# Splitting each chunk of two expert tables by one 1024-wide instruction instead of two 512-wide ones

## The chip and what is measured

The kernel runs on one core of a Trainium2 chip. The metric is the device time of one execution in microseconds. A core has the engines TensorE (PE in the rows; its weight loads are PEld), VectorE (DVE), ScalarE (ACT), GpSimd (POOL) and SyncE (SP, which here issues the transfers), each with its own instruction stream. They wait for one another on semaphores.

## The reference

One layer of a small diffusion backbone on 256 tokens of width 1024: projections and attention first, then the part that this study is on, a retrieval feed-forward over 16384 experts:

```
s = jnp.einsum('thpd,hpkd->thpk', q, sub_keys)        # 8 heads x 2 lists x 128 keys
top_s, top_i = lax.top_k(s, 16)                        # then the 16 best of 16 x 16 pairs
best_s, best_pos = lax.top_k(cand_s, 16)
g = jax.nn.softmax(best_s, axis=-1)
act = jax.nn.gelu(einsum('thkd,td->thk', u_tab[expert], hb))
return einsum('thk,thkd->td', g * act, v_tab[expert])
```

## The kernel before

It doesn't gather. It goes over both tables whole (64 MB each), in 128 chunks of 128 experts x 1024 values, and gives an expert that wasn't chosen the weight zero. All of it is fp32. To have nearly fp32 accuracy at the speed of the reduced fp32 format, each matrix is split into a high part (rounded) and a low part (the rest), and each product is three matmuls: hi x hi, hi x lo, lo x hi.

A chunk's way, in the names of the code:
- SyncE brings it from HBM into `stage`, which has four slots of [128, 1024]. A slot is filled again once the low part of the chunk in it is made (`lo_made`).
- ScalarE rounds it into `hi` (`round_chunk`, L939), when `stage_full` of the slot has come and TensorE has consumed what stood there (`piece_done`).
- VectorE subtracts into `lo` (`rest`, L1306), once `hi_made` has come.
- TensorE uses both and counts `piece_done`.

`hi` and `lo` hold four pieces of 512 columns each, so two chunks. Three stretches follow one another:
- **u**, chunks 0 to 63 of the first table: 24 matmuls of 256 columns a chunk (`u_chunk`, L788 to L790), and ScalarE's gelu on the chunk before the last (L1062). VectorE finds the top 16 of heads 4 to 7 between chunks (`choose`), then decodes them to expert numbers by 2048-wide instructions (L1454, L1459, L1463) with two chunks between each, and the softmax comes at the end.
- **u beside gates**, chunks 64 to 127: the same, and before each chunk four products that spread the gates over all experts (`gates`, L798), for which ScalarE and VectorE build one-hot rows (L1081, L1087, L1495).
- **v**, the 128 chunks of the second table: 12 matmuls of 512 columns a chunk (`v_chunk`, L851 to L853), which add up over all chunks in four banks. The weights of this product, gates times gelu, are split too, into `w_hi` (ScalarE, L1117) and `w_lo` (VectorE, L1535), two chunks deep, shown as h_hi and h_lo in the rows.

The order on each engine is written out by hand in the code; in the loops it is the order of the statements, and each engine runs its own in order.

Of the kernel before, what the change touches and what calls it, by code (L numbers as in the profile page):

```python
# [1 line left out]

# [28 lines left out]
LOWEST = -3.0e38  # L51
SLOTS = 4
CHUNKS = NK
PIECE = D // 2
PIECES = 4
GT = 4
GROUPS = T // GT

# [197 lines left out]
def build(nc, x_t, ctx_t, cols, rows, sgu_gain, final_gain, constants, sgu_wt, bias_mask, ada_w, w_in,  # L256
# [21 lines left out]
    with ExitStack() as stack:  # L278
# [82 lines left out]
        bias = sbuf("stage", [P, SLOTS, D])  # L361
        stage = bias
        BM = bias[:, :, :].rearrange("p s d -> p (s d)").rearrange("p (h b n) -> p h b n", h=HEADS, b=TB)
        hi = sbuf("hi", [P, PIECES, PIECE], F32R)
        lo = sbuf("lo", [P, PIECES, PIECE], F32R)
        h2_hi = sbuf("h2_hi", [P, KD, T], F32R)
        h2_lo = sbuf("h2_lo", [P, KD, T], F32R)
        with ExitStack() as views:
# [103 lines left out]
        @block.sync  # L472
        def _(sp):
            sp.dma_start(colv[:, :], cols).then_inc(cols_in, 16)
            sp.dma_start(X1, x_t).then_inc(x_in, 16)
            sp.dma_start(con[:, :], constants).then_inc(consts_in, 16)
            for n, (matrix, b) in enumerate(blocks):
                late = (matrix, b) in rings[1]
                slot = ring_of[(matrix, b)]
                if slot >= RING:  # L480
                    old = place[last_read(rings[late][slot - RING])]
                    sp.wait_ge(bank_full[old[0]], old[1] + 1)
                elif late:
                    old = place[("attend", 3)]
                    sp.wait_ge(bank_full[old[0]], old[1] + 1)
                sp.dma_start((WR2 if late else WR)[:, slot % RING], sources[matrix][b])\
                  .then_inc(ring_full[late][slot % RING], 16)
                if n == 2 * RING + 1:
                    sp.dma_start(C0, ctx_t).then_inc(ctx_in, 16)
                if n == RING - 1:  # L490
                    sp.dma_start(sgb_row, rows[:, 0:SGU_G * P]).then_inc(gating_in, 16)
                    sp.dma_start(sg_gain, sgu_gain).then_inc(gating_in, 16)
                    sp.dma_start(swt, sgu_wt).then_inc(gating_in, 16)

                if (matrix, b) == ("w_q", PH - 1):
                    old, use = place[("w_q", 2)]
                    sp.wait_ge(bank_full[old], use + 1)
                    for j in range(SLOTS):
                        sp.dma_start(stage[:, j, :], peer_u_t[j]).then_inc(stage_full[j], 16)
                if n == 27:  # L500
                    sp.dma_start(BM, bias_mask).then_inc(bias_in, 16)
                    sp.wait_ge(h_ready, KD)
                    sp.dma_start(SK, subkeys_t).then_inc(subkeys_in, 16)
                if (matrix, b) == ("w_q", 0):
                    sp.wait_ge(yr_ready, 1)
                    sp.dma_start(g2_row, rows[:, SGU_G * P:]).then_inc(g2_row_in, 16)
            with sp.Fori(1, CHUNKS // SLOTS) as i:
                for j in range(SLOTS):
                    sp.wait_ge(lo_made, i * (2 * SLOTS) + (2 * (j + 1 - SLOTS)))
                    sp.dma_start(stage[:, j, :], peer_u_t[i * SLOTS + j]).then_inc(stage_full[j], 16)  # L510
            with sp.Fori(0, CHUNKS // SLOTS) as i:
                for j in range(SLOTS):
                    sp.wait_ge(lo_made, i * (2 * SLOTS) + (2 * (CHUNKS + j + 1 - SLOTS)))
                    sp.dma_start(stage[:, j, :], v_rows[i * SLOTS + j]).then_inc(stage_full[j], 16)
            sp.wait_ge(gates_done, GROUPS)
            sp.dma_start(fin, final_gain).then_inc(fin_in, 16)
            for n in range(2 * TB):
                tb, half = n // 2, slice(n % 2 * 512, n % 2 * 512 + 512)
                sp.wait_ge(out_ready, n + 1)
                sp.dma_start(out[tb * P:(tb + 1) * P, half], x1n[:, tb, half]).then_inc(stored, 16)  # L520
            sp.wait_ge(stored, 16 * 2 * TB)
# [3 lines left out]
        def _(pe):  # L525
# [255 lines left out]

            def u_chunk(j, c):
                o = bank[j % SLOTS][:, 0:T]
                for h in range(2):
                    pe.wait_ge(lo_made, c * 2 + (h + 1))
                    for n in range(KD // 2):
                        k, p, kk = KD // 2 * h + n, (2 * j + h) % PIECES, slice(n * P, (n + 1) * P)
                        pe.matmul(o, hi[:, p, kk], h2_hi[:, k, :], start=(k == 0), stop=False)  # L788
                        pe.matmul(o, hi[:, p, kk], h2_lo[:, k, :], start=False, stop=False)  # L789
                        mm = pe.matmul(o, lo[:, p, kk], h2_hi[:, k, :], start=False, stop=(k == KD - 1))  # L790
                    mm.then_inc(piece_done, 1)


            def gates(j, g):
# [46 lines left out]
            def v_chunk(j, v, first=False, last=False):  # L841
                pe.wait_ge(wlo_made, v + 1)

                order = [(tb, half) for half in range(2) for tb in range(TB)]
                for n, (tb, half) in enumerate(sorted(order) if last else order):
                    if last or n % TB == 0:
                        pe.wait_ge(lo_made, v * 2 + (2 * CHUNKS + half + 1))
                    p = (2 * j + half) % PIECES
                    o = bank[4 + 2 * tb + half][:, :]
                    tt = slice(tb * P, (tb + 1) * P)  # L850
                    pe.matmul(o, w_hi[:, j % 2, tt], hi[:, p, :], start=first, stop=False)  # L851
                    pe.matmul(o, w_hi[:, j % 2, tt], lo[:, p, :], start=False, stop=False)  # L852
                    mm = pe.matmul(o, w_lo[:, j % 2, tt], hi[:, p, :], start=False, stop=last)  # L853
                    if last:
                        mm.then_inc(out_full, 1)
                    elif n % TB == TB - 1:
                        mm.then_inc(piece_done, 1)

            pe.wait_ge(gated, GROUPS)
            pe.wait_ge(choice_t_ready, 2 * TB)  # L860
# [27 lines left out]
        def _(act):  # L888
# [42 lines left out]
            def round_chunk(j, use, done=None):  # L931


                for h in range(2):
                    if done is not None:
                        act.wait_ge(piece_done, done + h)
                    if h == 0:
                        act.wait_ge(stage_full[j], use)
                    act.activation(hi[:, (2 * j + h) % PIECES, :], stage[:, j, h * PIECE:(h + 1) * PIECE], ACT.Copy)\  # L939
                       .then_inc(hi_made, 1)  # L940

            def round_h2(k):
                act.wait_ge(h2_ready, k + 1)
# [126 lines left out]

            def u_steps(i, j):

                round_chunk(j, i * 16 + 16, i * (2 * SLOTS) + (2 * j - 3))
                gelu_chunk(j - 2, i * SLOTS + (j - 2))

            def one1_squares(j, g, reused=True):
# [10 lines left out]
                act.activation(ONE1[:, j % 2], ONE1[:, j % 2], ACT.Relu, bias=1.0, scale=-1.0).then_inc(one1_made, 1)  # L1087

            for c in (2, 3):
                round_chunk(c, 16, 2 * c - 3)  # L1090
                gelu_chunk(c - 2, c - 2)
            with act.Fori(1, DECODE_UNTIL // SLOTS) as i:
                for j in range(SLOTS):
# [7 lines left out]
            for j in range(SLOTS):  # L1101
                c = MERGE + j
                one1_squares(j, j, reused=j >= 2)
                round_chunk(j, 16 * (c // SLOTS) + 16, 2 * c - 3)
                one1_rest(j, j)
                if j < 2:
                    gelu_chunk(j + 2, c - 2)
# [2 lines left out]
            with act.Fori(1, (CHUNKS - MERGE) // SLOTS) as i:  # L1110
                for j in range(SLOTS):
                    one1_squares(j, i * SLOTS + j)
                    round_chunk(j, i * 16 + (16 * (MERGE // SLOTS) + 16), i * (2 * SLOTS) + (2 * (MERGE + j) - 3))
                    one1_rest(j, i * SLOTS + j)
                    gelu_beside(j + 2, i * SLOTS + (j - 2))
            def w_round(j, v):
# [2 lines left out]

            for j in range(2):  # L1120
                n = CHUNKS + j
                round_chunk(j, 16 * (n // SLOTS) + 16, 2 * n - 3)
                gelu_beside(j + 2, n - 2 - MERGE)
                if j == 0:

                    act.wait_ge(gated, GROUPS)
                    act.wait_ge(piece_done, 2 * CHUNKS)
                w_round(j, j)


            act.wait_ge(multiplied, CHUNKS - MERGE)
            for v in (2, 3):
                act.wait_ge(piece_done, 2 * (CHUNKS + v - 1))
                w_round(v, v)
                round_chunk(v, 16 * (CHUNKS // SLOTS) + 16, 2 * (CHUNKS + v) - 3)
            with act.Fori(1, CHUNKS // SLOTS) as i:
                for j in range(SLOTS):
                    act.wait_ge(piece_done, i * (2 * SLOTS) + 2 * (CHUNKS + j - 1))
                    w_round(j, i * SLOTS + j)
                    round_chunk(j, i * 16 + (16 * (CHUNKS // SLOTS) + 16), i * (2 * SLOTS) + (2 * (CHUNKS + j) - 3))  # L1140

# [12 lines left out]
        def _(dve):  # L1156
# [143 lines left out]


            def rest(j, c):
                for h in range(2):
                    p = (2 * j + h) % PIECES
                    dve.wait_ge(hi_made, c * 2 + (h + 1))
                    dve.tensor_tensor(lo[:, p, :], stage[:, j, h * PIECE:(h + 1) * PIECE], hi[:, p, :].bitcast(F32),  # L1306
                                      ALU.subtract).then_inc(lo_made, 1)

            for kind, n in steps:
                if kind == "group" and n < 2:  # L1310
# [363 lines left out]
```

## Time and profile before

| what | value |
|---|---|
| median of 3 runs | 1107.93 us (1102.68 to 1108.59) |
| span of the profiled execution | 1106.2 us |
| its own time | not recorded apart from the span |
| TensorE busy | 1072.4 us, 97% of the span |
| VectorE busy | 760.1 us, 69% |
| ScalarE busy | 628.5 us, 57% |
| on the chain that ended last | TensorE 92%, ScalarE 3%, transfers 2%, VectorE 2% |

The chain that ended last is followed back from the last instruction, at each step to what released it. Busy time of TensorE is modelled from starts and a pipeline's length, so a matmul of 256 columns is shown as 0.28 us while the next one starts 0.12 us after it.

### The profile page before, as it was taken

What the parts mean: (1) busy time and instruction counts of PE and PEld (TensorE: products, weight loads), DVE (VectorE), ACT (ScalarE), POOL (GpSimd) and SP (SyncE); (2) the same over time, 40 slices, a digit from 0 to 9 for tenths busy, and PEclk for the clock granted to TensorE, in tenths of its full rate; (3) what the DMA queues carried; (4) which work ended last, traced back from release to release, by engine and by line L of the source; (5) the groups of instructions that cost most, each with busy time, mean ns of one, the idle gap of its engine ahead of it and who ended that gap; (6) DMA issues with size and microseconds to landing.
All of it is one profiled execution on the core that took longest, in us unless ns stands there. A gap on an engine that the chain in (4) does not pass through costs nothing.

```text
span 1106.2 us, 22735 instructions
## 1 busy us (share of the span) xinstructions
PE 1072.4 (97%) x7358; PEld 962.5 (87%) x7358; DVE 760.1 (69%) x1660; ACT 628.5 (57%) x1319; POOL 37.1 (3%) x11
## 2 busy tenths in 40 slices
PE   5899999999999999999999999999999999999996
PEld 3687986797999999999999999997888888888885
DVE  1373145576988878868888888886666666666666
ACT  2452235545345555578888888875555555555554
POOL 0000000003340000020000000000000000000000
PEclk9698998999999999999999999999999999999998
DMA  9665741044525555555344344445555666666653
GB/s 362 274 234 197 268 159 57 1 154 152 228 78 190 175 188 173 187 183 161 133 140 144 133 140 144 133 133 174 196 197 192 190 191 192 194 197 192 190 191 113
DMA packets 45547, 191.65 MB, mean 173 GB/s; under 512 B 5186, under 2 KB 5314, under 8 KB 38980
## 3 DMA queue, kind: packets, MB, share of 16 engines
q1 hardware_dynamic: 45508, 191.11, 50.9%
q8 instruction: 26, 0.43, 0.2%
q14 instruction: 13, 0.11, 0.0%
HBM read 190.04 MB, written 1.05 MB: 173 GB/s over the span
## 4 chain that ended last, share of the span: by engine, by line
PE 92%; ACT 3%; DMA 2%; DVE 2%; POOL 0%; issue 0%; DVEq 0%; SPq 0%; ACTq 0%
PE bank L788 11%; PE bank L789 11%; PE bank L790 11%; PE bank L851 10%; PE bank L853 10%; PE bank L852 10%; PE bank L798 5%; PE bank L546 3%; PE bank L547 3%; PE bank L548 3%; PE bank L669 2%; PE bank L566 1%; PE bank L652 1%; PE bank L651 1%; PE bank L660 1%; PE bank L556 1%
## 5 line engine op out<-in xcount | busy, mean ns | idle before, releaser
L939 ACT ACTIVATE hi<-stage 128x512 fp32r<-128x512 f32 x512 | 305.7, 622 | 119.6 <-PE bank L790 119.5
L1306 DVE TENSOR_TENSOR lo<-stage,hi 128x512 fp32r<-128x512 f32 x512 | 336.2, 695 | 33.9 <-ACT hi L939 31.4
L788 PE MATMUL bank<-h_hi,hi 128*128 128x256 f32 x1024 | 295.1, 288 | 1.0 <-ACT A L1062 1.0
L790 PE MATMUL bank<-h_hi,lo 128*128 128x256 f32 x1024 | 289.6, 283 | 0.0
L789 PE MATMUL bank<-h_lo,hi 128*128 128x256 f32 x1024 | 289.5, 283 | 0.0
L851 PE MATMUL bank<-hi,h_hi 128*128 128x512 f32 x512 | 199.3, 389 | 1.2 <-DVE h_lo L1535 1.2
L853 PE MATMUL bank<-hi,h_lo 128*128 128x512 f32 x512 | 199.2, 389 | 0.0
L852 PE MATMUL bank<-lo,h_hi 128*128 128x512 f32 x512 | 199.2, 389 | 0.0
L788 PEld LDWEIGHTS bank<-h_hi,hi 128*128 128x128 f32 x1024 | 196.1, 192 | 1.1 <-ACT A L1062 1.1
L789 PEld LDWEIGHTS bank<-h_lo,hi 128*128 128x128 f32 x1024 | 196.3, 192 | 0.0
L790 PEld LDWEIGHTS bank<-h_hi,lo 128*128 128x128 f32 x1024 | 196.0, 191 | 0.0
L1117 ACT ACTIVATE h_hi<-A 128x256 fp32r (+1 forms) x128 | 53.5, 418 | 162.4 <-PE bank L853 159.5
L1535 DVE TENSOR_TENSOR h_lo<-A,h_hi 128x256 fp32r<-128x256 f32 x128 | 54.5, 426 | 129.4 <-ACT h_hi L1117 129.4
L851 PEld LDWEIGHTS bank<-hi,h_hi 128*128 128x128 f32 x512 | 96.1, 188 | 21.2 <-issue 1.4
L852 PEld LDWEIGHTS bank<-lo,h_hi 128*128 128x128 f32 x512 | 96.1, 188 | 20.1
L853 PEld LDWEIGHTS bank<-hi,h_lo 128*128 128x128 f32 x512 | 96.1, 188 | 19.9
L1081 ACT ACTIVATE gate_buf<-con,choice_t 128x128 f32<-128x128 f32 x256 | 81.2, 390 | 0.0
L548 PE MATMUL bank<-h_hi,ring_low 128*128 128x256 f32 x256 | 72.6, 284 | 0.0
L1495 DVE TENSOR_SCALAR gate_buf<-con,choice_t 128x128 f32<-128x128 f32 x256 | 71.0, 340 | 0.0
L798 PE MATMUL bank<-gate_buf 128*128 128x128 f32 x512 | 67.6, 275 | 0.0
L798 PEld LDWEIGHTS bank<-gate_buf 128*128 128x128 f32 x512 | 62.8, 192 | 0.0
L1503 DVE TENSOR_TENSOR A<-A,bank 128x512 f32 (+1 forms) x64 | 43.9, 687 | 10.4 <-PE bank L798 1.8
(222 smaller groups left out, 1365.8 us busy)
## 6 DMA issues: line engine op xcount, KB each, us to landing
stage<-in_peer_u_t SPq DMA_DIRECT2D x128, 512.0 KB, 3.3
stage<-in_peer_v SPq DMA_DIRECT2D x128, 512.0 KB, 3.6
A<-in_ada_w SPq DMA_DIRECT2D x24, 1024.0 KB, 7.5
A<-in_w_in SPq DMA_DIRECT2D x11, 1024.0 KB, 4.8
A<-in_w_q SPq DMA_DIRECT2D x8, 1024.0 KB, 5.2
A<-in_w_out SPq DMA_DIRECT2D x4, 1024.0 KB, 7.3
stage<-in_bias_mask SPq DMA_DIRECT2D x1, 2048.0 KB, 12.9
A<-in_x_t SPq DMA_DIRECT2D x1, 1024.0 KB, 5.3
```

The costliest lines, as they stand in the source:

```text
L548: mm = pe.matmul(o, a_lo, b_hi, start=False, stop=(k == KD - 1))
L788: pe.matmul(o, hi[:, p, kk], h2_hi[:, k, :], start=(k == 0), stop=False)
L789: pe.matmul(o, hi[:, p, kk], h2_lo[:, k, :], start=False, stop=False)
L790: mm = pe.matmul(o, lo[:, p, kk], h2_hi[:, k, :], start=False, stop=(k == KD - 1))
L798: mm = pe.matmul(bank[4 + j][:, t * NK:(t + 1) * NK], ONE1[:, j, t, :], ONE2[:, j, t, :], start=True, stop=True)
L851: pe.matmul(o, w_hi[:, j % 2, tt], hi[:, p, :], start=first, stop=False)
L852: pe.matmul(o, w_hi[:, j % 2, tt], lo[:, p, :], start=False, stop=False)
L853: mm = pe.matmul(o, w_lo[:, j % 2, tt], hi[:, p, :], start=False, stop=last)
L939: act.activation(hi[:, (2 * j + h) % PIECES, :], stage[:, j, h * PIECE:(h + 1) * PIECE], ACT.Copy)\
L1081: last = act.activation(ONE1[:, j % 2, t, :], iota, ACT.Square, bias=choice_t[:, 0, bass.ds(g * GT + t, 1)])
L1306: dve.tensor_tensor(lo[:, p, :], stage[:, j, h * PIECE:(h + 1) * PIECE], hi[:, p, :].bitcast(F32), ALU.subtract).then_inc(lo_made, 1)
L1495: last = dve.tensor_scalar(ONE2[:, j % 2, t, :], iota, choice_t[:, 1, bass.ds(tt, 1)], choice_t[:, 2, bass.ds(tt, 1)], ALU.is_equal, ALU.mult)
```

## The change

Each chunk is rounded by one 1024-wide instruction and its rest is taken by one 1024-wide instruction. `hi` and `lo` are two tiles of a whole chunk, in the same space. The semaphores `hi_made`, `lo_made` and `piece_done` count chunks, where they counted halves. The matmuls, their order in a chunk but for which tile they name, and everything else stay.

```diff
-PIECE = D // 2
-PIECES = 4
+TILES = 2
-        hi = sbuf("hi", [P, PIECES, PIECE], F32R)
-        lo = sbuf("lo", [P, PIECES, PIECE], F32R)
+        hi = sbuf("hi", [P, TILES, D], F32R)
+        lo = sbuf("lo", [P, TILES, D], F32R)
@@ SyncE
-                    sp.wait_ge(lo_made, i * (2 * SLOTS) + (2 * (j + 1 - SLOTS)))
+                    sp.wait_ge(lo_made, i * SLOTS + (j + 1 - SLOTS))
@@ TensorE, u_chunk
-                for h in range(2):
-                    pe.wait_ge(lo_made, c * 2 + (h + 1))
-                    for n in range(KD // 2):
-                        k, p, kk = KD // 2 * h + n, (2 * j + h) % PIECES, slice(n * P, (n + 1) * P)
-                        pe.matmul(o, hi[:, p, kk], h2_hi[:, k, :], start=(k == 0), stop=False)
-                        pe.matmul(o, hi[:, p, kk], h2_lo[:, k, :], start=False, stop=False)
-                        mm = pe.matmul(o, lo[:, p, kk], h2_hi[:, k, :], start=False, stop=(k == KD - 1))
-                    mm.then_inc(piece_done, 1)
+                pe.wait_ge(lo_made, c + 1)
+                for k in range(KD):
+                    kk = slice(k * P, (k + 1) * P)
+                    pe.matmul(o, hi[:, j % TILES, kk], h2_hi[:, k, :], start=(k == 0), stop=False)
+                    pe.matmul(o, hi[:, j % TILES, kk], h2_lo[:, k, :], start=False, stop=False)
+                    mm = pe.matmul(o, lo[:, j % TILES, kk], h2_hi[:, k, :], start=False, stop=(k == KD - 1))
+                mm.then_inc(piece_done, 1)
@@ TensorE, v_chunk
+                pe.wait_ge(lo_made, v + (CHUNKS + 1))
-                    if last or n % TB == 0:
-                        pe.wait_ge(lo_made, v * 2 + (2 * CHUNKS + half + 1))
-                    elif n % TB == TB - 1:
-                        mm.then_inc(piece_done, 1)
+                if not last:
+                    mm.then_inc(piece_done, 1)
@@ ScalarE, round_chunk
-                for h in range(2):
-                    if done is not None:
-                        act.wait_ge(piece_done, done + h)
-                    if h == 0:
-                        act.wait_ge(stage_full[j], use)
-                    act.activation(hi[:, (2 * j + h) % PIECES, :], stage[:, j, h * PIECE:(h + 1) * PIECE], ACT.Copy)\
-                       .then_inc(hi_made, 1)
+                if done is not None:
+                    act.wait_ge(piece_done, done)
+                act.wait_ge(stage_full[j], use)
+                act.activation(hi[:, j % TILES, :], stage[:, j, :], ACT.Copy).then_inc(hi_made, 1)
@@ ScalarE, u: first half needs piece 2c-3, now the whole needs chunk c-1 of the count
-                round_chunk(j, i * 16 + 16, i * (2 * SLOTS) + (2 * j - 3))
+                round_chunk(j, i * 16 + 16, i * SLOTS + (j - 1))
@@ VectorE, rest
-                for h in range(2):
-                    p = (2 * j + h) % PIECES
-                    dve.wait_ge(hi_made, c * 2 + (h + 1))
-                    dve.tensor_tensor(lo[:, p, :], stage[:, j, h * PIECE:(h + 1) * PIECE], hi[:, p, :].bitcast(F32),
-                                      ALU.subtract).then_inc(lo_made, 1)
+                dve.wait_ge(hi_made, c + 1)
+                dve.tensor_tensor(lo[:, j % TILES, :], stage[:, j, :], hi[:, j % TILES, :].bitcast(F32),
+                                  ALU.subtract).then_inc(lo_made, 1)
```

What stands on ScalarE in one turn of the loop of v, before (ISA is a separate instruction that only waits):

```order
L1117 ISA [waits piece_done]
L1117 ACTIVATE h_hi<-A 128x256
L936 REGISTER_ALU
L939 ACTIVATE hi<-stage 128x512 [waits stage_full1,piece_done]
L939 ACTIVATE hi<-stage 128x512 [waits piece_done]
```

And in the changed kernel (its line numbers are lower, since blank lines at its head are gone):

```order
L1112 REGISTER_ALU
L1091 ISA [waits piece_done]
L1091 ACTIVATE h_hi<-A 128x256
L914 ACTIVATE hi<-stage 128x1024 [waits stage_full1,piece_done]
L1112 REGISTER_ALU
```

Two instructions became one; the wait for consumed weights still stands ahead of all of them.

On VectorE, in the decoding at the end of u, four halves (two chunks) stand between two 2048-wide instructions before:

```order
L1454 TENSOR_TENSOR A<-A,con 128x2048
L1306 TENSOR_TENSOR lo<-stage,hi 128x512 [waits hi_made,dve_done]
L1306 TENSOR_TENSOR lo<-stage,hi 128x512 [waits hi_made] x3
L1459 TENSOR_TENSOR A<-A 128x2048
L1306 TENSOR_TENSOR lo<-stage,hi 128x512 [waits hi_made,dve_done]
```

In the changed kernel these four are two 1024-wide ones, at the same place.

## Rows read from the trace of the kernel before

**Rows 1.** The page's first line.

```profile
span 1106.2 us, 22735 instructions
```

**Rows 2.** Windows: stretch, length; busy PE, PEld, DVE, ACT, POOL; clock; DMA share; GB/s.

```profile
319.00:500.00 181.00, 180.03 (x1502) 179.86 (x1502) 148.62 (x352) 102.77 (x193) 13.90 (x2) 1.00 0.54 176
500.00:747.00 247.00, 246.84 (x2097) 246.63 (x2095) 216.61 (x514) 201.60 (x518) 0.00 (x0) 1.00 0.43 140
748.00:1095.00 347.00, 346.94 (x1531) 287.40 (x1532) 217.52 (x383) 186.64 (x383) 0.00 (x0) 1.00 0.59 189
```

**Rows 3.** Groups by form: count, busy us, mean ns, idle before.

```profile
L939 ACT ACTIVATE hi<-stage 128x512 fp32r<-128x512 f32 x512 | 305.7, 622 | 119.6 <-PE bank L790 119.5
L956 ACT ACTIVATE hi<-A 128x2048 fp32r<-128x2048 f32 x6 | 11.5, 1912 | 18.5 <-DMA A<-in_w_in 18.4
L1240 DVE TENSOR_TENSOR ring_low<-A,hi 128x2048 fp32r<-128x2048 f32 x6 | 13.8, 2292 | 39.6 <-ACT hi L956 39.5
```

**Rows 4.** Timeline of v, one turn: start, length, engine, line, idle before.

```profile
851.83 0.42 ACT L1117 ACTIVATE h_hi<-A 128x256 fp32r x1 [1.26 <-PE bank L853]
852.15 1.14 ACT L939 ACTIVATE hi<-stage 128x512 fp32r<-128x512 f32 x2
852.80 1.29 DVE L1306 TENSOR_TENSOR lo<-stage,hi 128x512 fp32r<-128x512 f32 x2
854.25 0.39 PE L851 MATMUL bank<-hi,h_hi 128*128 128x512 f32 x1
...
854.55 0.42 ACT L1117 ACTIVATE h_hi<-A 128x256 fp32r x1 [1.26 <-PE bank L853]
```

**Rows 5.** Timeline of u, in the decoding.

```profile
448.24 0.69 DVE L1306 TENSOR_TENSOR lo<-stage,hi 128x512 fp32r<-128x512 f32 x1 [0.34 <-ACT hi L939]
448.85 2.29 DVE L1454 TENSOR_TENSOR A<-A,con 128x2048 f32<-128x2048 uint32 x1
...
450.45 0.63 ACT L939 ACTIVATE hi<-stage 128x512 fp32r<-128x512 f32 x1 [0.81 <-PE bank L790]
451.17 2.08 DVE L1306 TENSOR_TENSOR lo<-stage,hi 128x512 fp32r<-128x512 f32 x3
...
453.13 0.28 PE L788 MATMUL bank<-h_hi,hi 128*128 128x256 f32 x1
...
453.33 0.63 ACT L939 ACTIVATE hi<-stage 128x512 fp32r<-128x512 f32 x1 [0.81 <-PE bank L790]
```

**Rows 6.** Timeline of VectorE in u, around one step of top-k.

```profile
388.37 0.08 DVE L1265 MATCH_VALUE_LOAD top_i<-top_v,A 128x8 f32 x1
...
390.46 1.28 DVE L1306 TENSOR_TENSOR lo<-stage,hi 128x512 fp32r<-128x512 f32 x2
```

**Rows 7.** Timeline of u, where TensorE waited.

```profile
329.10 2.83 DVE L1306 TENSOR_TENSOR lo<-stage,hi 128x512 fp32r<-128x512 f32 x2
...
332.11 0.36 PE L788 MATMUL bank<-h_hi,hi 128*128 128x256 f32 x1 [0.97 <-ACT A L1062]
...
332.31 0.28 PE L789 MATMUL bank<-h_lo,hi 128*128 128x256 f32 x1
```

**Rows 8.** Timeline of the stage before u, a wait of TensorE.

```profile
256.03 0.42 DVE L1401 TENSOR_TENSOR h_lo<-A,h_hi 128x256 fp32r<-128x256 f32 x1
...
256.50 0.39 PE L546 MATMUL bank<-h_hi,query_hi 128*128 128x256 f32 x1
```

**Rows 9.** Timeline of ScalarE in u, around the softmax.

```profile
479.02 1.28 ACT L939 ACT_TABLE_LOAD   x1
...
489.41 1.28 ACT L939 ACT_TABLE_LOAD   x1 [0.61 <-PE bank L790]
```

**Rows 10.** Timeline of u beside gates.

```profile
603.75 0.63 ACT L939 ACTIVATE hi<-stage 128x512 fp32r<-128x512 f32 x1 [0.65 <-PE bank L790]
...
604.36 0.36 PE L788 MATMUL bank<-h_hi,hi 128*128 128x256 f32 x1
```

**Rows 11.** Transfers of the page: count, KB each, us from issue to landing.

```profile
stage<-in_peer_v SPq DMA_DIRECT2D x128, 512.0 KB, 3.6
```

More of the change, by code:

```diff
@@ L512, in _ @@
                 for j in range(SLOTS):
-                    sp.wait_ge(lo_made, i * (2 * SLOTS) + (2 * (CHUNKS + j + 1 - SLOTS)))
+                    sp.wait_ge(lo_made, i * SLOTS + (CHUNKS + j + 1 - SLOTS))
                     sp.dma_start(stage[:, j, :], v_rows[i * SLOTS + j]).then_inc(stage_full[j], 16)
@@ L842, in v_chunk @@
                 pe.wait_ge(wlo_made, v + 1)
+                pe.wait_ge(lo_made, v + (CHUNKS + 1))
                 order = [(tb, half) for half in range(2) for tb in range(TB)]
-                for n, (tb, half) in enumerate(sorted(order) if last else order):
-                    if last or n % TB == 0:
-                        pe.wait_ge(lo_made, v * 2 + (2 * CHUNKS + half + 1))
-                    p = (2 * j + half) % PIECES
+                for tb, half in sorted(order) if last else order:
+                    dd = slice(half * 512, half * 512 + 512)
                     o = bank[4 + 2 * tb + half][:, :]
                     tt = slice(tb * P, (tb + 1) * P)
-                    pe.matmul(o, w_hi[:, j % 2, tt], hi[:, p, :], start=first, stop=False)
-                    pe.matmul(o, w_hi[:, j % 2, tt], lo[:, p, :], start=False, stop=False)
-                    mm = pe.matmul(o, w_lo[:, j % 2, tt], hi[:, p, :], start=False, stop=last)
+                    pe.matmul(o, w_hi[:, j % 2, tt], hi[:, j % TILES, dd], start=first, stop=False)
+                    pe.matmul(o, w_hi[:, j % 2, tt], lo[:, j % TILES, dd], start=False, stop=False)
+                    mm = pe.matmul(o, w_lo[:, j % 2, tt], hi[:, j % TILES, dd], start=False, stop=last)
                     if last:
                         mm.then_inc(out_full, 1)
-                    elif n % TB == TB - 1:
-                        mm.then_inc(piece_done, 1)
+                if not last:
+                    mm.then_inc(piece_done, 1)
             pe.wait_ge(gated, GROUPS)
@@ L1089, in _ @@
             for c in (2, 3):
-                round_chunk(c, 16, 2 * c - 3)
+                round_chunk(c, 16, c - 1)
                 gelu_chunk(c - 2, c - 2)
@@ L1103, in _ @@
                 one1_squares(j, j, reused=j >= 2)
-                round_chunk(j, 16 * (c // SLOTS) + 16, 2 * c - 3)
+                round_chunk(j, 16 * (c // SLOTS) + 16, c - 1)
                 one1_rest(j, j)
@@ L1112, in _ @@
                     one1_squares(j, i * SLOTS + j)
-                    round_chunk(j, i * 16 + (16 * (MERGE // SLOTS) + 16), i * (2 * SLOTS) + (2 * (MERGE + j) - 3))
+                    round_chunk(j, i * 16 + (16 * (MERGE // SLOTS) + 16), i * SLOTS + (MERGE + j - 1))
                     one1_rest(j, i * SLOTS + j)
@@ L1121, in _ @@
                 n = CHUNKS + j
-                round_chunk(j, 16 * (n // SLOTS) + 16, 2 * n - 3)
+                round_chunk(j, 16 * (n // SLOTS) + 16, n - 1)
                 gelu_beside(j + 2, n - 2 - MERGE)
@@ L1126, in _ @@
                     act.wait_ge(gated, GROUPS)
-                    act.wait_ge(piece_done, 2 * CHUNKS)
+                    act.wait_ge(piece_done, CHUNKS)
                 w_round(j, j)
@@ L1132, in _ @@
             for v in (2, 3):
-                act.wait_ge(piece_done, 2 * (CHUNKS + v - 1))
+                act.wait_ge(piece_done, CHUNKS + v - 1)
                 w_round(v, v)
-                round_chunk(v, 16 * (CHUNKS // SLOTS) + 16, 2 * (CHUNKS + v) - 3)
+                round_chunk(v, 16 * (CHUNKS // SLOTS) + 16, CHUNKS + v - 1)
             with act.Fori(1, CHUNKS // SLOTS) as i:
                 for j in range(SLOTS):
-                    act.wait_ge(piece_done, i * (2 * SLOTS) + 2 * (CHUNKS + j - 1))
+                    act.wait_ge(piece_done, i * SLOTS + (CHUNKS + j - 1))
                     w_round(j, i * SLOTS + j)
-                    round_chunk(j, i * 16 + (16 * (CHUNKS // SLOTS) + 16), i * (2 * SLOTS) + (2 * (CHUNKS + j) - 3))
+                    round_chunk(j, i * 16 + (16 * (CHUNKS // SLOTS) + 16), i * SLOTS + (CHUNKS + j - 1))
             act.activation(fsum[:, 2, TB:TB + 1], eps[:, :], ACT.Sqrt)
```

## The prediction

> **What bounds the kernel now.** I read the windows by stage first. The end of the kernel is made of three long stretches [rows 2]: u, chunks 0 to 63 of the first table (319 to 500 us); u beside gates, chunks 64 to 127 (500 to 747); v, the 128 chunks of the second table (748 to 1095). TensorE is busy for 180.03 of 181, 246.84 of 247 and 346.94 of 347 us, at a granted clock of 1.00, while ScalarE and VectorE have gaps everywhere. So TensorE sets the time, and it is idle for 0.97 + 0.16 + 0.06 = 1.2 us in all. Nothing that the split into parts costs now is on the path; the question is only whether it stays off.
>
> The timeline then tells how close it is. hi and lo hold two chunks, so chunk c can be rounded only once chunk c-2 has been consumed, and it must be ready when chunk c-1 is consumed. In v [rows 4] ScalarE is released by chunk v-2 at 851.83, does the weight tile w_hi (0.32 us until the next starts), then both halves of hi from 852.15; VectorE starts lo at 852.80; TensorE starts chunk v at 854.25. The next turn starts at 854.55, so a chunk takes 2.72 us. Between release and need there are 854.25 - 851.83 = 2.42 us. In u [rows 5] they are 453.13 - 450.45 = 2.68 us, and a chunk takes 24 matmuls of 0.12 us, 2.88 us (450.45 to 453.33, the next release).
>
> **What the change removes and adds.** By pieces, hi's second half runs on ScalarE while lo's first half runs on VectorE, and TensorE needs only lo's first half to begin. Whole chunks put the full hi and the full lo one behind the other ahead of TensorE. In u they also take away an early start: so far the first half is released half a chunk sooner, when half of chunk c-2 is consumed.
>
> Duration of the new instructions. No row has a 1024-wide one. On a line between the 512-wide and the 2048-wide rows [rows 3], ScalarE: 0.622 + (1.912 - 0.622)/3 = 1.05 us; VectorE, from the single lo of 0.69 us [rows 5]: 0.69 + (2.292 - 0.69)/3 = 1.22 us. Bounds: not under the start-to-start time of halves, not over two halves back to back (1.14 and 1.29 us, [rows 4]). The first lo starts 0.03 us after the first hi ends (852.15 + 0.62).
>
> TensorE's restart. In v it hardly ever waits, so I take it from the one wait on lo in u [rows 7]: lo ends at 329.10 + 2.83 = 331.93, the matmul starts at 332.11, and the one after it at 332.31, 0.08 later than the 0.12 of a running row. Together 0.26 us. The lower bound is in an earlier stage [rows 8]: VectorE ends at 256.45, TensorE starts at 256.50 with a matmul of 0.39 where 0.28 is usual, together 0.16. I take 0.26: same line, same kind of wait, inside a loop.
>
> **v.** From release to TensorE's start: 0.32 + 1.05 + 0.03 + 1.22 + 0.26 = 2.88 us, where 2.42 are to be had. Late by 0.46 us. The wait ties chunk v to the end of chunk v-2, so the delay comes once in two chunks: 63 pairs x 0.46 = **29.0 us**. With 0.16 for the restart 0.36 x 63 = 23; with nothing for it 0.20 x 63 = 13.
>
> In v ScalarE and VectorE are busy for 187 and 218 of 347 us [rows 2]. The Trainium skill (Perfetto Trace Analysis, Optimizing Scalar/DVE Operations) says that grouping operations helps where such an engine is saturated, and that where it is not but causes bubbles elsewhere, breaking instructions up lets work be done sooner. This change goes against the second half of it. By that rule too the time rises; how much, the page doesn't say, and the sum is from the rows alone.
>
> **u.** With VectorE free: 1.05 + 0.03 + 1.22 + 0.26 = 2.56 us against 2.68, so 0.12 us are left and nothing is lost. But VectorE is not always free. Its lo of chunk c would end at 450.45 + 2.30 = 452.75. Then
> - decoding: a 2048-wide instruction follows every two chunks, 12 in all (L1454, L1459 and L1463, four each). It starts 0.08 before the end of the lo ahead (448.85 against 448.24 + 0.69) and the next lo 2.32 after it (451.17), [rows 5]. Then lo of chunk c+1 ends at 452.67 + 2.32 + 1.22 = 456.21, TensorE starts by 456.47, and needed it at 453.13 + 2.88 = 456.01. 12 x 0.46 = **5.5 us**. Now the first half of that lo is the one needed, half a chunk's time ahead of it, and this hides it.
> - top-k: the longest of the eight steps of a head takes 2.09 us (388.37 to 390.46, [rows 6]); by the same sum 0.23 us late, for 4 heads **0.9 us**. The other steps are short enough.
> - ScalarE's table loads around the softmax. hi is due on a beat of 2.88 us from 450.45: at 479.25 and at 490.77. The first is held up by a load until 479.02 + 1.28 = 480.30 [rows 9], and by 1.05 - 0.62 = 0.43 more since the hi ahead is longer: 1.48 - 0.12 = 1.4 us. The second load stands between the wait and hi, 1.28 - 0.12 = 1.2 us. Together **2.5 us**. Today they fall on a first half with half a chunk to spare.
>
> Sum of u: 8.9 us. Below it the restart of 0.16 gives 12 x 0.36 + 0.5 + 2.3 = 7. Above it: if the chain in u is over 0.12 us longer than I have it, nearly every pair of its 64 chunks waits. At 0.3 us late this is 32 x 0.3 = 10 us more.
>
> **u beside gates.** hi is released at 603.75 and chunk c-1 starts at 604.36 [rows 10]. lo is done and TensorE could start at 603.75 + 2.56 = 606.31; TensorE is on chunk c-1 until 604.36 + 2.88 = 607.24 and then has gates. 0.9 us to spare without the gates. ScalarE and VectorE there are busy 202 and 217 of 247 us, and each loses a start per chunk. Nothing, either way.
>
> **Transfers.** A slot of stage is released when the whole lo is made, before and after; that comes some 0.4 us later. There are four slots and a transfer takes 3.6 us [rows 11] out of the three chunk times (over 8 us) that it has. Hidden.
>
> **Sum.** 29.0 + 8.9 = 37.9 us. The profiled execution's span is 1106.2 us [rows 1]; the median of three runs is 1107.9, 1.7 above it, which I put to what lies around the span. 1106.2 + 37.9 + 1.7 = 1145.8 us, say 1146 (+3.4%). The runs of before spread over 5.9 us, so about 0.5% is what can be told from no change.
>
> **The rivals.**
> - *The chain fits in v: no change.* If hi and lo together take no more than 2.42 us from release, TensorE never waits in v. It decides at 0.46 less than my 2.88: the restart at nothing (0.26) and 0.20 off the two instructions. The start-to-start times speak a little for it (a lo starts 0.60 after the one ahead though it is shown as 0.69). Then u's few waits stay at most: 1108 to 1115 us. For 1108 sharp, within 0.5%, u's have to vanish too. 11% in all, 4 of them for the second.
> - *Saved starts pay: as now or faster.* Per chunk ScalarE saves 1.14 - 1.05 = 0.09 us and VectorE 0.07. This pays only where TensorE waits for them, and that is 1.2 us in 775 [rows 2]: 1106 to 1108 us. Against it: that idle time is all there is to win. 3%. The Trainium skill (VectorE: DVE Perf Modes, on the TRN2 errata) says that each instruction pays a fixed extra latency, and advises large tiles. The fixed part agrees with the rows (two halves cost more than the whole on the line); the advice, by the idle time above, buys nothing here.
> - *u is tied as well.* The 0.12 us of u are used up (one loop turn in four starts hi behind a separate waiting instruction, which is new to the path): 10 us more, 1156 us. 15%.
> - *The clock falls.* If TensorE's gaps of 0.46 us in 5.9 brought the granted clock below 1.00, v alone would grow by tens of us. Against it: the gaps stay short, and TensorE is busy over 90% of the time. 2%.
> - My forecast, v tied pairwise and u at a few places: 69%.
>
> **How the numbers follow.** The likeliest case with its bounds runs from 1107.9 + 13 + 5 = 1126 to 1107.9 + 29 + 9 + 4 = 1150; the one tied in u reaches to 1160. I leave out the two rivals at 1115 and below and the clock, 16% in all, so the range is 1127 to 1160. Slower by over 0.5%: 69 + 15 + 2 and most of the 7, 0.91; within 0.5%: 0.07; faster: 0.02.
>
> **What would show it.** ScalarE's 1024-wide hi at 1.05 us and VectorE's lo at 1.22. In v, TensorE waits for VectorE's lo some 63 times (or 126 times, half as long), 15 to 29 us in all by idle time alone, and a pair of chunks takes 5.90 us where it took 5.44; VectorE no longer idles beside a full TensorE. In u, waits at the 12 decoding instructions and at two table loads, and a plain chunk still at 2.88 us. u beside gates keeps its 247 us within 1. The prediction is wrong if the pair in v stays at 5.44 (the chain is shorter than the rows say), or if plain chunks of u stretch.

## The result: 2.9% slower

Before 1107.1 us (median), after 1138.0: a ratio of 1.0289, 95% interval 1.0256 to 1.0322. The forecast was 1146 in 1127 to 1160.

The profiled execution went from 1106.2 to 1134.5 us. Its page's lines that answer to [rows 1] and [rows 3], for the changed kernel:

```profile
span 1134.5 us, 21582 instructions
...
PE 73%; DVE 11%; ACT 9%; DMA 3%; issue 3%; ACTq 0%; POOL 0%; DVEq 0%; SPq 0%
...
L1278 DVE TENSOR_TENSOR lo<-stage,hi 128x1024 fp32r<-128x1024 f32 x256 | 314.8, 1230 | 119.6 <-ACT hi L914 119.0
L914 ACT ACTIVATE hi<-stage 128x1024 fp32r<-128x1024 f32 x256 | 269.1, 1051 | 142.7 <-PE bank L768 142.6
```

512 instructions of each engine became 256, and their busy time fell: ScalarE's from 305.7 to 269.1 us, VectorE's from 336.2 to 314.8. Yet the time rose. The chain that ended last was TensorE to 92% before; now it is TensorE to 73%, and ScalarE and VectorE hold 20% of it: making hi and lo has become work that the end of the program waits for.

Where it came from is read from the first and the last start of TensorE's lines. For the changed kernel (columns: least, median and greatest length in ns, then first and last start):

```profile
L766 PE MATMUL bank<-h_hi,hi x1024: 277/283/388, 316.5 to 748.9; 128*128 128x256 f32 x171
L776 PE MATMUL bank<-gate_buf x512: 272/275/275, 508.2 to 746.3; 128*128 128x128 f32 x171
L828 PE MATMUL bank<-hi,h_hi x512: 387/393/504, 750.6 to 1124.0; 128*128 128x512 f32 x171
```

u runs from the first of these to the second, and so on. The same three lines give every kernel of this study a length for each stretch:

| kernel | u | u beside gates | v |
|---|---|---|---|
| before | 186.2 | 242.5 | 347.5 |
| changed | 191.7 (+5.5) | 242.4 | 373.4 (+25.9) |

Together 31.3 us more. The part of the program ahead of u took 319.4 us in one profile and 316.5 in the other; over all profiles here it lies between 313.7 and 322.4 whatever the kernel, so single spans differ by some us for that alone, and the lengths of the stretches are the sharper measure (the same kernel parts agree within 0.1 or 0.2 us). The granted clock goes with it. In the profile of the kernel before it falls from 1.00 (2.4 GHz) to 0.50 (1.2 GHz) for 10 us from 168 us on. In that of the changed kernel it doesn't, though TensorE had been busy for 9.50 of the 10 us from 155 to 165 in both. The eight profiles with such a drop between 166 and 185 us start u at 317.3 us or later, the four without it at 316.5 or earlier.

The waits of TensorE after 320 us, longest first (us in total, times, longest):

```profile
PEld bank L828 <- DVE lo L1278: 33.5, 83, 0.5
...
PEld bank L766 <- DVE lo L1278: 2.9, 10, 0.6
PE bank L766 <- DVE lo L1278: 2.8, 4, 1.1
```

These are shown at the weight loads (PEld), which stand first at a chunk; before the change no such row named lo. The weight loads' idle time is more than what TensorE lost. The starts of v's 1536 matmuls, set against those of the kernel before, show 63 late starts, one at the head of every second chunk, and 14.8 us lost at them in all.

One pair of chunks in v, in the timeline of the changed kernel, answers to [rows 4]:

```profile
853.18 0.42 ACT L1091 ACTIVATE h_hi<-A 128x256 fp32r x1 [1.78 <-PE bank L830]
853.50 1.04 ACT L914 ACTIVATE hi<-stage 128x1024 fp32r<-128x1024 f32 x1
...
854.58 1.23 DVE L1278 TENSOR_TENSOR lo<-stage,hi 128x1024 fp32r<-128x1024 f32 x1 [0.42 <-ACT hi L914]
...
855.40 0.39 PE L830 MATMUL bank<-hi,h_lo 128*128 128x512 f32 x1
855.86 0.50 PE L828 MATMUL bank<-hi,h_hi 128*128 128x512 f32 x1
856.20 0.40 PE L829 MATMUL bank<-lo,h_hi 128*128 128x512 f32 x1
...
861.75 0.50 PE L828 MATMUL bank<-hi,h_hi 128*128 128x512 f32 x1
```

Read it as a relay. TensorE's end of a chunk releases ScalarE at 853.18; w_hi (h_hi in the row) comes first; hi from 853.50 to 854.54; lo from 854.58 to 855.81; TensorE starts 0.05 us later, at 855.86. It would have been ready one spacing after 855.40, at 855.63. The next such start is at 861.75: this pair takes 5.89 us, where one took 5.44. It is one of the longer ones; the mean of v's 63 pairs is 0.41 us above 5.44.

### The profile page after: what moved, and what is told of

It reads as the page before. It is cut to its first block, busy times and chain, and to the rows that moved or that the text cites. A ratio compares the mean times of both kernels' runs of the same rounds, so it can differ in the third digit from the quotient of the medians.

```text
span 1134.5 us, 21582 instructions
## 1 busy us (share of the span) xinstructions
PE 1092.9 (96%) x7358; PEld 952.6 (84%) x7358; DVE 742.6 (65%) x1404; ACT 598.3 (53%) x1063; POOL 37.0 (3%) x11
## 3 DMA queue, kind: packets, MB, share of 16 engines
HBM read 190.04 MB, written 1.05 MB: 168 GB/s over the span
## 4 chain that ended last, share of the span: by engine, by line
PE 73%; DVE 11%; ACT 9%; DMA 3%; issue 3%; ACTq 0%; POOL 0%; DVEq 0%; SPq 0%
PE bank L766 10%; PE bank L767 9%; PE bank L768 9%; DVE lo L1278 7%; PE bank L828 7%; PE bank L830 6%; PE bank L829 6%; ACT hi L914 6%; PE bank L776 5%; PE bank L525 3%; PE bank L527 3%; PE bank L526 3%; PE bank L648 1%; DMA A<-in_w_in 1%; PE bank L545 1%
## 5 line engine op out<-in xcount | busy, mean ns | idle before, releaser
L1278 DVE TENSOR_TENSOR lo<-stage,hi 128x1024 fp32r<-128x1024 f32 x256 | 314.8, 1230 | 119.6 <-ACT hi L914 119.0
L914 ACT ACTIVATE hi<-stage 128x1024 fp32r<-128x1024 f32 x256 | 269.1, 1051 | 142.7 <-PE bank L768 142.6
L828 PE MATMUL bank<-hi,h_hi 128*128 128x512 f32 x512 | 207.9, 406 | 5.9 <-DVE h_lo L1507 1.2
```

The lines of the kernel that those rows point to most:

```text
L828: pe.matmul(o, w_hi[:, j % 2, tt], hi[:, j % TILES, dd], start=first, stop=False)
L914: act.activation(hi[:, j % TILES, :], stage[:, j, :], ACT.Copy).then_inc(hi_made, 1)
L1278: dve.tensor_tensor(lo[:, j % TILES, :], stage[:, j, :], hi[:, j % TILES, :].bitcast(F32), ALU.subtract).then_inc(lo_made, 1)
```

## The experiments

**Theory 1** is that of the prediction: the full hi and the full lo stand one behind the other between the end of chunk c-2 and the need for chunk c, and this relay is longer than what TensorE has to do meanwhile. **Theory 2** has several forms: it is the coarser waiting and releasing by chunks, or one engine's long instruction by itself, or a disturbance of TensorE beside the relay. Ratios are to the kernel before, run on the same chip. The edits are against the changed kernel where nothing else is said.

### Only lo by halves

```diff
-                pe.wait_ge(lo_made, c + 1)
                 for k in range(KD):
+                    if k % (KD // 2) == 0:
+                        pe.wait_ge(lo_made, c * 2 + (k // (KD // 2) + 1))
...
-                dve.tensor_tensor(lo[:, j % TILES, :], stage[:, j, :], hi[:, j % TILES, :].bitcast(F32),
-                                  ALU.subtract).then_inc(lo_made, 1)
+                for s in (slice(0, D // 2), slice(D // 2, D)):
+                    dve.tensor_tensor(lo[:, j % TILES, s], stage[:, j, s], hi[:, j % TILES, s].bitcast(F32),
+                                      ALU.subtract).then_inc(lo_made, 1)
```

(and the same wait in v and on SyncE.)

> hi by one 1024-wide instruction as in the change, lo by two halves, TensorE waits by halves; TensorE's count of consumed chunks stays whole. Theory 1 (hi and lo stand one behind the other between the end of chunk v-2 and the need for chunk v): in v 0.32 + 1.05 + 0.04 + 0.69 + 0.05 = 2.15 us of 2.42, no wait; in u only the two table loads may still cost some 0.5 us each. 1107 to 1110 us. Theory 2 (the coarser release of consumed chunks, or the longer ScalarE instruction, costs it): both are still there, so most of the 31 us stay, 1125 to 1138.

Measured: 1108.3 us, ratio 1.0006 (0.9990 to 1.0022). u 188.0, v 347.7. ScalarE's single instruction and the release by chunks are still there and cost nothing in v. u keeps 1.8 us, where theory 1 had some 0.5 at each of two table loads. Its starts show 0.8 at the first table load (481.48) and nothing at the second; 0.5 at 446.07, where a 2048-wide reduce and three short VectorE instructions stand ahead of lo; and 0.4 more at the start of 330.41, at which the kernel before waits too (332.11). So the total lies in theory 1's range, and its places in u are right in part.

### Only hi by halves

```diff
-                act.activation(hi[:, j % TILES, :], stage[:, j, :], ACT.Copy).then_inc(hi_made, 1)
+                for s in (slice(0, D // 2), slice(D // 2, D)):
+                    act.activation(hi[:, j % TILES, s], stage[:, j, s], ACT.Copy).then_inc(hi_made, 1)
...
-                dve.wait_ge(hi_made, c + 1)
+                dve.wait_ge(hi_made, c * 2 + 2)
```

> The other way round: hi by two halves, lo by one 1024-wide instruction after both, all else as in the change. Theory 1: the chain has 1.14 us where it had 1.05, so 0.09 us more in each of 63 pairs and a little in u: 1138 + 6 = 1144 us, slower than the change. Theory 2 (the single long ScalarE instruction is what costs): back to near 1110.

Measured: 1145.6 us, ratio 1.0336 (1.0296 to 1.0375). u 192.8, v 379.0: 5.6 us more in v than the change, where 0.09 x 63 = 5.7 were expected. So going back to the old ScalarE instructions makes it worse when VectorE still waits for both.

### Both by halves, waits and releases by chunks

```diff
+                for s in (slice(0, D // 2), slice(D // 2, D)):
+                    act.activation(hi[:, j % TILES, s], stage[:, j, s], ACT.Copy).then_inc(hi_made, 1)
...
+                for h, s in enumerate((slice(0, D // 2), slice(D // 2, D))):
+                    dve.wait_ge(hi_made, c * 2 + (h + 1))
+                    last = dve.tensor_tensor(lo[:, j % TILES, s], stage[:, j, s], hi[:, j % TILES, s].bitcast(F32),
+                                             ALU.subtract)
+                last.then_inc(lo_made, 1)
```

> hi and lo both by halves as before the change, but TensorE waits for whole chunks and counts whole chunks as after it: only the overlap of ScalarE and VectorE inside a chunk comes back. Theory 1: lo would be whole at 854.09 + 0.05 where it is needed at 854.25 (times of before), no wait in v; in u the decoding instructions may cost up to 0.1 us each and the table loads 1 us each: 1108 to 1111 us. Theory 2 (waiting and releasing by whole chunks costs it, not the instructions): about 1138.

Measured: 1114.2 us, ratio 1.0058 (1.0043 to 1.0073): 3 us above what theory 1 gave, and far from theory 2. u 189.0, v 351.1. Of the change's 31.3 us, 6.4 are left in u and v. Waiting and releasing by whole chunks is thus the small part; giving up the overlap of the two engines inside a chunk is the large one. As for the 3.6 us of v that theory 1 did not have, TensorE waits for next to nothing there,

```profile
PEld bank L828 <- DVE lo L1280: 2.1, 13, 0.2
```

and yet its matmuls stand a little farther apart, by 0.229 us in the mean instead of 0.227 (see the last section).

### The weight tile taken out of the relay

```diff
-        w_hi = h2_hi[:, 0:2, :]
-        w_lo = h2_lo[:, 0:2, :]
+        w_hi = h2_hi[:, 0:4, :]
+        w_lo = h2_lo[:, 0:4, :]
...
-                    act.wait_ge(piece_done, i * SLOTS + (CHUNKS + j - 1))
                     w_round(j, i * SLOTS + j)
```

(w_hi and w_lo are addressed by j % 4 throughout.)

> The change as it is, but w_hi and w_lo are four chunks deep in v, so ScalarE makes w_hi ahead of its wait for TensorE. Theory 1: 0.32 us leave the chain, 1.05 + 0.04 + 1.22 + 0.05 = 2.36 us of 2.42 are left, v is back to 347 us or some 4 more, u keeps its 5.5: 1112 to 1117 us. Theory 2 (it is the long instructions by themselves, or how they disturb TensorE's matmuls): nothing changes, 1138.

Measured: 1116.8 us, ratio 1.0074 (1.0051 to 1.0098). u 191.7, v 352.0. The long instructions are all still there; ScalarE now makes w_hi ahead of time, the relay is 0.32 us shorter, and 21.4 of v's 25.9 us are gone. The timeline of this kernel:

```profile
855.87 1.06 ACT L914 ACTIVATE hi<-stage 128x1024 fp32r<-128x1024 f32 x1 [1.29 <-PE bank L830]
...
856.84 0.40 ACT L1091 ACTIVATE h_hi<-A 128x256 fp32r x1
...
856.96 1.23 DVE L1276 TENSOR_TENSOR lo<-stage,hi 128x1024 fp32r<-128x1024 f32 x1 [1.10 <-ACT hi L914]
```

hi is now what starts at TensorE's release, and h_hi (w_hi) follows it.

### A copy added to the relay, after and before the change

In the loop of v, after w_round; nothing reads what it writes:

```diff
                     w_round(j, i * SLOTS + j)
+                    act.activation(h2_hi[:, 4 + j % 2, :], A3[:, i * SLOTS + j, :], ACT.Copy)
```

> The change with one more 256-wide ScalarE copy per chunk in the loop of v, between w_hi and hi, into a place that nothing reads. Theory 1: the chain is 0.32 us longer and TensorE waits for it once in a pair of chunks, so v grows by 62 x 0.32 = 20 us from 373.4 to 393 us; 1158 us. Theory 2 (TensorE is slowed by something that stands beside the chain, ScalarE having 40% of v free): the copy is hidden, 1138 us.

> The same copy put into the kernel before the change. Theory 1: lo's first half would be made at 852.80 + 0.32 + 0.69 = 853.81 where it is needed at 854.25, and the second at 854.41 where it is needed at 855.6: hidden, v stays at 347.5 us, 1107 to 1109 us. Theory 2 (any 0.32 us on ScalarE in v costs): as much as in the run above, 1127 us.

Measured in the changed kernel: 1155.3 us, ratio 1.0424 (1.0387 to 1.0460), v 392.0, which is 18.6 us more than without it. In the timeline the copy pushes hi back by 0.30 us,

```profile
851.91 0.40 ACT L1114 ACTIVATE h_hi<-A 128x256 fp32r x1
852.21 1.05 ACT L914 ACTIVATE hi<-stage 128x1024 fp32r<-128x1024 f32 x1
```

and 62 x 0.30 = 18.6 (the loop with the copy has 62 pairs): what is added to the relay is paid once in a pair, in full. In the kernel before: 1107.7 us, ratio 0.9993 (0.9971 to 1.0016), v 347.6. Hidden.

### Two and three copies in the kernel before

```diff
+                    for n in range(2):       # 3 in the other run
+                        act.activation(h2_hi[:, 2 + n + 3 * (j % 2), :], A3[:, i * SLOTS + j, :], ACT.Copy)
```

> Kernel before the change with two of the 256-wide ScalarE copies per chunk in the loop of v (0.30 us each, as the run with one in the changed kernel showed). Theory 1: lo's first half is made at 853.49 + 0.60 = 854.09, TensorE is told at 854.14, just ahead of the 854.25 at which it needs it: no wait, v between 347.5 and 352 us (the two runs that were this close showed 351.1 and 352.0). 1107 to 1112 us. Theory 2 (the cover in v is about as thin as the one copy, whole chunks or not): 10 us or more.

> The same with three copies. Theory 1: lo's first half is made at 854.39, told at 854.44, 0.19 us late, and a restart costs 0.11 more: 0.30 us in each of 62 pairs, 18.6 us: v 366 us, 1126 us. So the kernel before obeys the same sum, with 0.7 us more of cover. Theory 2 (only whole-chunk instructions make TensorE wait): v at most 352 us, 1112 us.

Measured: 1111.3 us with two (ratio 1.0038, 1.0016 to 1.0060), v 350.9; 1127.7 us with three (1.0202, 1.0152 to 1.0251), v 370.2. Both answers of theory 1, with v 4 us over its sum in the second. The waits of TensorE at lo in v appear with them, at 512-wide instructions: with two copies, then with three,

```profile
PEld bank L851 <- DVE lo L1308: 12.9, 79, 0.2
```

```profile
PEld bank L851 <- DVE lo L1308: 28.9, 61, 0.5
```

By the starts of the matmuls, no chunk is late with two copies and 62 are with three, 13.7 us in all, one in each pair of the loop. So whole-chunk instructions aren't needed to make TensorE wait. The kernel before had some 0.7 us of cover in v, and the change spends it and 0.24 us more in each pair.

### Whole chunks in u alone

SyncE's, TensorE's and VectorE's waits in v count halves again, and round_chunk has a parameter:

```diff
-            def round_chunk(j, use, done=None):
+            def round_chunk(j, use, done=None, parts=1):
...
+                for n in range(parts):
+                    s = slice(n * D // parts, (n + 1) * D // parts)
+                    act.activation(hi[:, j % TILES, s], stage[:, j, s], ACT.Copy).then_inc(hi_made, 1)
```

> Whole chunks in both stretches of the first table, halves as before in v. Theory 1: the parts add up: v is back at 347.5 us, u keeps 191.7 us (186.2 before), gates 242.5: 1107 + 5.5 = 1112.5 us (1110 to 1115). Theory 2 (the loss in v comes from how u leaves the queues and buffers): v stays near 373 us, 1138.

Measured: 1112.3 us, ratio 1.0055 (1.0034 to 1.0076). u 191.7, gates 242.5, v 347.6. The two losses are separate and add up.

### The decoding's instructions by halves

```diff
-                    another()
-                    another()
-                    link(dve.tensor_tensor(b3, digit[:, p, :].unsqueeze(2).broadcast_to([P, PH * TOPK, TOPK]),
-                                           iota16, ALU.is_equal))
+                    halves = [(slice(64 * q, 64 * q + 64), slice(4 * q, 4 * q + 4)) for q in range(2)]
+                    for ms, hs in halves:
+                        another()
+                        link(dve.tensor_tensor(b3[:, ms, :], digit[:, p, ms].unsqueeze(2).broadcast_to([P, 64, TOPK]),
+                                               iota[:, 0:TOPK].unsqueeze(1).broadcast_to([P, 64, TOPK]), ALU.is_equal))
```

(and so for the multiply and the reduce.)

> The change with the twelve 2048-wide VectorE instructions of the decoding made by halves of 1024, one after each chunk instead of one after two. Theory 1: lo of the next chunk then ends at 452.67 + 1.24 + 1.22 = 455.1 where it is needed at 456.0 (times of before), so the waits of TensorE beside the decoding go and those at the table loads stay: u takes 191.7 - 2.5 = 189.2 us. Theory 2 (u loses by the longer chain everywhere, a little per chunk): u stays at 191.7.

Measured by one profile: u 189.4, v 373.5. Of the waits beside the decoding one of 0.2 us is left (425.44); those at the table loads and at top-k are there still. A small loss, placed.

## Why the prediction held, and where it was off

**What bounds it, and the relay.** Right. TensorE was the bound with 1.2 us idle, and became the one that waits. The relay is release, w_hi, hi, lo, start. The runs above took w_hi out, put a copy in, and made hi and lo longer or shorter; each time v moved as the sum said, but for the 3 to 4.5 us of the last section.

**The new instructions.** 1.05 and 1.22 us forecast, 1.051 and 1.230 measured. The line between the 512- and the 2048-wide rows was good to 1%.

**v: 29.0 us forecast, 25.9 measured.** The tie was as forecast: 63 late starts, one in each pair. The starts of all matmuls of v, set against the kernel before, divide the 25.9 us: 14.8 at the late starts themselves (0.24 each, relay and first part of the restart), 6.9 at the matmul after each (0.11 more: 0.34 after the first where 0.23 is usual), and 4.2 at all the others, which stand 0.230 us apart where they stood 0.227. Two terms were off, in opposite ways. The restart, put at 0.26, is 0.16 in v: 0.05 from lo's end to TensorE's start and the 0.11, as in [rows 8], from which the prediction had its lower bound. With 0.16 the sum gives 23 us, and 14.8 + 6.9 is 21.7. The slower matmuls had no term. So the total came nearer than its parts, which is partly luck.

The 0.26 of [rows 7] was read rightly, but the place is of a rarer kind. Of the thirteen waits on lo in u of the changed kernel, ten have 0.05 and 0.10. The same place again, 329.67, where lo ends at 329.49 beside GpSimd's memset, has 0.18 and 0.07, and the two at table loads have 0.15 and 0.07. What makes these three differ isn't shown.

**u: 8.9 us forecast, 5.5 measured.** The places were right. The gaps between TensorE's starts in u, over its 0.12 us of the running row and less those of the kernel before, account for 5.4 us. There are 2.5 us beside the decoding (5.5 forecast). Top-k costs 1.0 (0.9 forecast): 0.23 at three heads and 0.36 at the first (322.62), where hi is done at 320.74 and VectorE comes to lo only at 321.36. The two table loads cost 1.9 (2.5 forecast): 1.35 at the first (1.4) and 0.56 at the second (1.2), where six other matmuls, which the sum left out, fill part of the wait:

```profile
495.44 0.82 PE L798 MATMUL bank<-con,choice 128*128 128x128 f32 x6
```

The term that was mis-sized most is the decoding, "12 x 0.46". Six places wait, not twelve. Five cost 0.37 us, and one 0.62, where three short VectorE instructions stand between the 2048-wide one and lo. The timeline of the changed kernel shows why:

```profile
455.48 2.29 DVE L1431 TENSOR_TENSOR A<-A 128x2048 f32<-128x2048 f32 x1
457.80 1.23 DVE L1278 TENSOR_TENSOR lo<-stage,hi 128x1024 fp32r<-128x1024 f32 x1
...
459.08 0.39 PE L766 MATMUL bank<-h_hi,hi 128*128 128x256 f32 x1
...
460.10 1.23 DVE L1278 TENSOR_TENSOR lo<-stage,hi 128x1024 fp32r<-128x1024 f32 x1 [1.07 <-ACT hi L914]
461.24 2.28 DVE L1435 TENSOR_REDUCE choice<-A 128x128 f32<-128x2048 f32 x1
463.56 1.23 DVE L1278 TENSOR_TENSOR lo<-stage,hi 128x1024 fp32r<-128x1024 f32 x1
```

The lo of 457.80 ends at 459.03, and TensorE, which would have been ready at 458.81, starts at 459.08. But the next hi was released by the chunk that had ended before this delay, so the next 2048-wide instruction starts (461.24) as if there had been none, and the lo after it (463.56) is in time for a TensorE that is now 0.37 us behind. One delay pays for two instructions. I had added up twelve independent delays; a delay on TensorE gives everybody else that much time, once.

**u beside gates and the transfers: nothing.** Right: 242.4 us against 242.5, and no wait for `stage`.

**The rivals.** That the relay fits in v: it doesn't, by 0.24 us ahead of the 0.11 at the second matmul; with w_hi out of it, it does. That saved starts pay: 36.6 and 21.4 us of busy time were saved, and nothing came of them. That u is tied all along: plain chunks still take 2.88 us. The clock: the granted clock stays at 1.00 (2.4 GHz) in v.

The Trainium skill (Perfetto Trace Analysis, Optimizing Scalar/DVE Operations) had both halves of this: larger operations for a saturated engine, and smaller ones, which may help, where an unsaturated engine makes bubbles on another. The runs agree with the second for lo, whose halves bring the ratio from 1.0289 to 1.0006. Halving hi alone makes it 1.0336, since VectorE still waits for both halves: a split pays where the next engine can start on the first part.

No version here beats the kernel before: its TensorE has 1.2 us idle in these stretches, and the run with hi whole and lo by halves ties with it.

## What to carry to other kernels

Where two engines hand a tile on to a third, write down the time from the release of the buffer to the need for it, and lay the whole relay beside it, with everything that stands ahead of it on the first engine (here a small tile of 0.32 us decided 21 us). Fewer, larger instructions save busy time on engines that have it to spare and lengthen the relay by what used to overlap. When late places follow one another, don't add them: the first delay on the bounding engine is slack for the next.

## What the runs showed of the hardware

TensorE's rate goes, by a little, with how far ahead its waits are fulfilled. The lead here is the time from the end of the lo that a chunk of v waits for to the chunk's start. The copies on ScalarE in the kernel before change it, and leave the instructions for hi and lo and the waits as they are: without a copy it is 0.76 us, with one 0.45, with two 0.16, and v takes 347.6, 347.6 and 350.9 us (by unrounded starts). The other kernels fall in line. With only lo by halves the lead is 0.33 and v takes 347.7. With halves and waits by chunk it is 0.18 and v takes 351.1; with the deep weight tile it is 0.19 or 0.25, by turns, and v takes 352.0.

In the three slow ones the first matmul of a chunk is never more than 0.03 us late, though the weight loads show 2.1 to 12.9 us of idle time until lo. The 3.2 to 4.4 us in 1536 matmuls are 2 to 3 ns each, and they aren't spread evenly. With halves and waits by chunk the matmuls of a chunk follow one another after 0.233, 0.232, 0.230 and 0.229 us at first, and after 0.227 from the eighth on, up to the wait of the next chunk (0.229); in the kernel before it is 0.226 to 0.227 at every place. So in these rows TensorE takes some seven matmuls after such a wait to come back to 0.227. Which part of the way to a matmul this is was not settled. For a plan it means that "just in time" is some 1% late.
